# The chunk matrices of the recurrence as 64x64 diagonal blocks, multiplied in quarters of the TensorE array

## What is computed

```python
def step(S, inp):
    r_t, w_t, k_t, v_t, a_t, b_t = inp
    sa = jnp.einsum('bhvk,bhk->bhv', S, a_t)
    S = S * w_t[:, :, None, :] + sa[..., None] * b_t[:, :, None, :] + v_t[..., None] * k_t[:, :, None, :]
    y = jnp.einsum('bhvk,bhk->bhv', S, r_t)
    return S, y
...
_, ys = lax.scan(step, S0, xs)          # 256 steps, 16 heads, S is 64x64 for each head
...
y = ((y - mean) * lax.rsqrt(var + GN_EPS)).reshape(B, T, D_RWKV)
...
return (y + bonus.reshape(B, T, D_RWKV)) * g
```

## Time and profile before

| what | value |
|---|---|
| median of three executions | 2832.23 us (2830.13 to 2838.66) |
| profiled execution: its time | 2842.54 us |
| profiled execution: span of its instructions | 2840.8 us |
| PE busy | 2535.0 us (89% of the span) |
| DVE busy | 1992.4 us (70%) |
| ACT busy | 1122.2 us (40%) |
| granted TensorE clock, mean | 0.938 of 2.4 GHz |

### The profile page before, as it was taken

One profiled execution on the slowest core, in us unless ns is written; L12 is line 12 of the kernel. 1 busy time (PEld: TensorE's weight loads), 2 busy tenths in 40 slices (PEclk: granted clock), 3 DMA queues, 4 the chain that ended last, 5 costly groups with the idle time before them and its releaser, 6 DMA issues.

```text
span 2840.8 us, 49508 instructions
## 1 busy us (share of the span) xinstructions
PE 2535.0 (89%) x20356; PEld 2457.9 (87%) x20356; DVE 1992.4 (70%) x2444; ACT 1122.2 (40%) x1179; POOL 96.5 (3%) x184
## 2 busy tenths in 40 slices
PE   1298996889999999999889998998899999999997
PEld 1298973889999999999788887888899999999997
DVE  6877776578887778777778776866678754465644
ACT  1143332345554324443344343342455543344433
POOL 1000000000000000000000000000000000000000
PEclk7599995999999999999999989999899999999999
DMA  9776860567776877777657231320477545455543
GB/s 385 292 298 252 331 258 15 191 239 271 289 292 261 322 282 285 284 281 286 262 208 268 89 125 36 119 104 20 164 280 269 218 163 187 169 192 180 190 164 117
DMA packets 87613, 613.58 MB, mean 216 GB/s; under 512 B 9545, under 2 KB 13137, under 8 KB 14033
## 3 DMA queue, kind: packets, MB, share of 16 engines
q1 hardware_dynamic: 64320, 443.22, 42.5%
q0 software_dynamic: 23184, 168.83, 15.4%
HBM read 607.80 MB, written 4.21 MB: 215 GB/s over the span
## 4 chain that ended last, share of the span: by engine, by line
PE 81%; DVE 12%; issue 4%; ACT 2%; DMA 0%; DVEq 0%; SPq 0%; ACTq 0%
PE ps L645 23%; PE ps L647 23%; PE ps L646 23%; PE ps L642 1%; PE ps L550 1%; DVE ada_raw L1438 1%; DVE w_lo L1425 1%; DVE inv_t L1339 1%; PE ps L566 1%; DVE tmp L1463 1%; DVE w_lo L1421 1%; DVE h_lo L1467 1%; PE ps L767 1%; DVE rstd L1455 1%; PE ps L447 1%
## 5 line engine op out<-in xcount | busy, mean ns | idle before, releaser
L645 PE MATMUL ps<-h_hi,w_hi 128*128 128x256 f32 x4480 | 1273.1, 284 | 165.7 <-DVE w_lo L1421 111.2
L647 PE MATMUL ps<-h_hi,w_lo 128*128 128x256 f32 x4480 | 1268.3, 283 | 0.0
L646 PE MATMUL ps<-h_lo,w_hi 128*128 128x256 f32 x4480 | 1262.8, 282 | 0.0
L1421 DVE TENSOR_TENSOR w_lo<-w_raw,w_hi 128x2048 fp32r<-128x2048 f32 x323 | 740.2, 2292 | 532.0 <-ACT w_hi L953 531.0
L953 ACT CAST w_hi<-w_raw 128x2048 fp32r<-128x2048 f32 x323 | 617.0, 1910 | 1052.0 <-PE ps L647 1027.6
L645 PEld LDWEIGHTS ps<-h_hi,w_hi 128*128 128x128 f32 x4480 | 857.4, 191 | 173.8 <-issue 143.4
L646 PEld LDWEIGHTS ps<-h_lo,w_hi 128*128 128x128 f32 x4480 | 857.6, 191 | 0.4
L647 PEld LDWEIGHTS ps<-h_hi,w_lo 128*128 128x128 f32 x4480 | 856.3, 191 | 0.0
L645 PE MATMUL ps<-hid_hi,w_hi 128*128 (+1 forms) x1408 | 396.8, 282 | 21.8 <-issue 21.8
L646 PE MATMUL ps<-hid_lo,w_hi 128*128 (+1 forms) x1408 | 397.0, 282 | 0.0
L647 PE MATMUL ps<-hid_hi,w_lo 128*128 (+1 forms) x1408 | 396.2, 281 | 0.0
(11 more groups left out here) (334 smaller groups left out, 1831.2 us busy)
## 6 DMA issues: line engine op xcount, KB each, us to landing
w_raw<-in_w_stream SPq DMA_DIRECT2D x376, 1024.0 KB, 4.8
ada_raw<-in_ada_stream POOLq DMA_DIRECT2D x160, 1024.0 KB, 6.5
w_raw<-in_ada_stream SPq DMA_DIRECT2D x32, 1024.0 KB, 4.8
x<-in_x_t SPq DMA_DIRECT2D x1, 2048.0 KB, 18.2
x_kept<-x SPq DMA_DIRECT2D x1, 2048.0 KB, 8.3
x<-x_kept SPq DMA_DIRECT2D x1, 2048.0 KB, 7.7
out_t<-x SPq DMA_DIRECT2D x4, 512.0 KB, 2.6
ada_c<-in_c SPq DMA_DIRECT2D x1, 1024.0 KB, 4.9
```

Of the source, the lines that this page charges most:

```text
L645: mm(o, hi, r_hi, start=first, stop=False, **kw)
L646: mm(o, hi, r_lo, start=False, stop=False, **kw)
L647: return mm(o, lo, r_hi, start=False, stop=last, **kw)
L1421: tt(w_lo[:, slot], w_raw[:, slot], w_hi[:, slot % 2].bitcast(F32), ALU.subtract).then_inc(lo_ready, 1)
```

## The change

The chunk matrices shrink from 128x128 to two stacked 64x64 blocks (`mats`, `n_low`, `inv`, `inv_t`, and the mask constants). Every matmul on them is cut into matmuls of 64 rows and 64 columns, one for each block (`HALVES`). The products of both heads come in one go, four quarters in turn, so that the PE no longer waits for DVE between the heads. DVE handles all four matrices of a group in one instruction of half the width, and `mats` is masked last, after everything that the first level needs. The transposes move from ahead of level 0 into it, and the `mats` products with the values move from level 4 to level 2. The outputs are 16 quarter matmuls for a group instead of 8 of 128 rows. The sequence over the chunks (5) has the same matmuls as before. Line numbers of the tensor and vector programs move by up to 16.

```diff
-CONSTS = [("ident", 128), ("ones", 128), ("head64", 128), ("low0", 128), ("up0", 128), ("lev", 5 * 128),
-          ("strict_low", 128), ("mask2", 256), ("tri", 256), ("scan", 256), ("recip", 1024)]
+CONSTS = [("ident", 128), ("ones", 128), ("head64", 128), ("low0", 64), ("up0", 64), ("lev", 5 * 64),
+          ("strict_low", 64), ("mask3", 3 * 64), ("ident64", 64), ("tri", 256), ("scan", 256), ("recip", 1024)]
...
-                mats = [sb(t, f"mats{i}", [P, 4, 3, P]) for i in range(2)]
-                n_low = [sb(t, f"n_low{i}", [P, 4, P]) for i in range(2)]
-                inv = [sb(t, f"inv{i}", [P, 4, P]) for i in range(2)]
-                inv_t = [sb(t, f"inv_t{i}", [P, 4, P]) for i in range(2)]
+                mats = [sb(t, f"mats{i}", [P, 4, 3, CHUNK]) for i in range(2)]
+                n_low = [sb(t, f"n_low{i}", [P, 4, CHUNK]) for i in range(2)]
+                inv = [sb(t, f"inv{i}", [P, 4, CHUNK]) for i in range(2)]
+                inv_t = [sb(t, f"inv_t{i}", [P, 4, CHUNK]) for i in range(2)]
...
+        HALVES = [slice(0, 64), slice(64, P)]
+
+        def by_chunk(t):
+            return t.rearrange("p (w t) -> p w t", w=4)
...
-            for e in range(2):
-                rows = slice(64 * e, 64 * e + 64)
-                for s, g, b in both:
-                    BT, KTL = wk[s][:, 5], wk[s][:, 4]
-                    if e:
-                        pe.wait_ge(S("masked"), of(i, 2, 0, s))
-                    else:
-                        pe.wait_ge(S("tilded"), g + 1)
-                    for t in range(2):
-                        tt = slice(P * t, P * t + P)
-                        mm(ps[:, b + t, 0:T], BT[rows, tt], ar[s][rows, :, tt], start=True, stop=True)
-                        mm(ps[:, b + t, T:512], KTL[rows, tt], ar[s][rows, :, tt], start=True, stop=True)
...
+            for s, g, b in both:
+                pe.wait_ge(S("tilded"), g + 1)
+                for t in range(2):
+                    for k, src in ((0, 5), (2, 4)):
+                        for h, p in enumerate(HALVES):
+                            for e, rows in enumerate(HALVES):
+                                tt = slice(P * t + 64 * h, P * t + 64 * h + 64)
+                                o = (4 * t + k) * 64
+                                mm(ps[p, b + e, o:o + P], wk[s][rows, src, tt], ar[s][rows, :, tt], start=True, stop=True)
...
             for m in range(5):
                 for s, g, b in both:
-                    NL = wtmp[s][:, 0:2].rearrange("p a (b t) -> p (a b) t", b=2)
+                    NL = by_chunk(wtmp[s][:, 0])
...
                     for w in range(4):
-                        last = mm(ps[:, b, w * P:w * P + P], NL[:, w], inv_t[s][:, w], start=True, stop=True)
+                        for p in HALVES:
+                            last = mm(ps[p, b + 2, w * 64:w * 64 + 64], NL[p, w], inv_t[s][p, w], start=True, stop=True)
                     last.then_inc(S("half"), 1)
...
+                for k, src, n in ((0, u_tok[s], 0), (1, tok[s][:, 2], 2)):
+                    for t in range(2):
+                        for h, p in enumerate(HALVES):
+                            for e, rows in enumerate(HALVES):
+                                last = mm(ps[rows, b + h, T + t * 64:T + t * 64 + 64], src[p, t, rows],
+                                          mats[s][p, 2 * e + t, n, :], start=k == 0 and t == 0, stop=k == 1 and t == 1,
+                                          skip_group_check=True)
...
-                    nc.scalar.copy(wtmp[s][:, 2:4].rearrange("p a t -> p (a t)"), ps[:, b, :]).then_inc(S("yt"), 1)
...
+                    nc.scalar.copy(wtmp[s][:, 2], ps[:, b + 2, 0:T]).then_inc(S("yt"), 1)
...
-                    last = tt(inv_t[s][:], inv_t[s][:], ps[:, b + 1, :].rearrange("p (w t) -> p w t", w=4), ALU.add)
+                    last = tt(inv_t[s][:], inv_t[s][:], by_chunk(ps[:, b + 1, 0:T]), ALU.add)
```

More of the change, by code:

```diff
@@ L118, in level, with within @@
         return (i // (2 << m) == j // (2 << m)) & (i % (2 << m) >= (1 << m)) & (j % (2 << m) < (1 << m))
[L120 to L125, removed]
+    def within(m):
+        return np.where(i < CHUNK, m[:, :CHUNK], m[:, CHUNK:])
+    put("low0", within(level(0)))
+    put("up0", within(level(0).T))
+    put("lev", np.concatenate([within(level(m)) for m in range(1, 6)], 1))
+    put("strict_low", within(j < i))
+    strict, incl = within(i < j), within(i <= j)
+    put("mask3", np.concatenate([incl, strict, incl], 1))
+    put("ident64", within(i == j))
     put("tri", i <= np.arange(T)[None, :])
@@ L483, in wkv_pe @@
         def wkv_pe(pe, mm, pair, i):
[L484 removed]
+            head64 = wk_const("head64", P)
             both = groups(i)
@@ new lines, in wkv_pe @@
+            for s, g, b in both:
+                pe.wait_ge(S("rk_read"), g + 1)
+            for s, g, b in both:
+                for t in range(2):
+                    for h, p in enumerate(HALVES):
+                        for e, rows in enumerate(HALVES):
+                            tt = slice(P * t + 64 * h, P * t + 64 * h + 64)
+                            o = T + P * s + 64 * t
+                            last = mm(ps[p, 4 + 3 * e, o:o + 64], ar[s][rows, 0, tt], wk[s][rows, 5, tt], start=True,
+                                      stop=True)
@@ L551, in wkv_pe @@
                     last.then_inc(S("half"), 1)
-                if m == 4:
+                if m == 0:
                     for s, g, b in both:
-                        pe.wait_ge(S("inv_ready"), of(i, 5, m, s))
+                        pe.wait_ge(S("masked"), g + 1)
+                        for n, src in enumerate((wk[s][:, 5], wk[s][:, 4])):
+                            for t in range(2):
+                                last = nc.tensor.transpose(ps[:, b, (2 * n + t) * P:(2 * n + t) * P + P],
+                                                           src[:, t * P:t * P + P], ident[:])
+                        last.then_inc(S("tok_turned"), 1)
@@ L556, in wkv_pe @@
+                if m == 2:
+                    for s, g, b in both:
+                        pe.wait_ge(S("tok"), g + 1)
                         for w in range(4):
                             e, t = w // 2, w % 2
-                            last = mm(ps[:, b + 2, (2 * t + e) * 64:(2 * t + e) * 64 + 64], mats[s][:, w, 1, :],
-                                      tok[s][:, 2, t, 64 * e:64 * e + 64], start=True, stop=True)
+                            for p in HALVES:
+                                last = mm(ps[p, b, (2 * t + e) * 64:(2 * t + e) * 64 + 64], mats[s][p, w, 1, :],
+                                          tok[s][p, 2, t, 64 * e:64 * e + 64], start=True, stop=True)
@@ L1326, in wkv_dve, with products @@
-            dve.wait_ge(S("masked"), of(i, 2, 1, 1))
+            def products(b):
+                return ps[:, b:b + 2, :].rearrange("p e (t k j) -> p (e t) k j", t=2, k=4)
+            dve.wait_ge(S("mats_mm"), i + 1)
+            for s, g, b in both:
+                o = T + P * s
+                tt(n_low[s][:].rearrange("p (e t) j -> p e t j", e=2),
+                   ps[:, 4:8:3, o:o + P].rearrange("p e (t j) -> p e t j", t=2),
+                   wk_const("strict_low").unsqueeze(1).unsqueeze(1).to_broadcast([P, 2, 2, CHUNK]),
+                   ALU.mult).then_inc(S("low_read"), 1)
+                steps.add(tt(inv_t[s][:], products(b)[:, :, 0], all4(wk_const("up0")), ALU.mult))
@@ L1333, in wkv_dve @@
             each(lambda s, g, b: tt(inv[s][:], n_low[s][:], all4(wk_const("low0")), ALU.mult))
             for s, g, b in both:
-                tt(inv[s][:], inv[s][:], all4(ident[:]), ALU.add).then_inc(S("inv_ready"), 1)
+                tt(inv[s][:], inv[s][:], all4(wk_const("ident64")), ALU.add).then_inc(S("inv_ready"), 1)
+            for s, g, b in both:
+                tt(mats[s][:].rearrange("p w k j -> p w (k j)"), products(b)[:, :, 1:4].rearrange("p w k j -> p w (k j)"),
+                   wk_const("mask3", 3 * CHUNK).unsqueeze(1).to_broadcast([P, 4, 3 * CHUNK]), ALU.mult).then_inc(S("masked"), 1)
```

87 lines of the change are left out of this document (30 added, 57 removed).

## The result

The median of four executions (one more of the kernel before than in the table above) went from 2834.09 us (2830.13 to 2838.66) to 2765.74 us (2764.61 to 2770.28): 0.9764 of the time before, with a 95% interval of 0.9750 to 0.9778, or 68 us less. The kernel is faster, by twice the 34 us that I forecast, and within the range given (2745 to 2828).

What follows compares the result with a forecast made beforehand. No transfer or single engine bounds the changed stretches; a chain between PE, DVE and ACT does. Head -6.3, levels -3.6, chunks +0.8, outputs -1.7, norm +2.2: -8.6 us a stage, -34 in all, 2798 us; range 2745 to 2828.

Steps and rivals of the forecast that it cites:

- The head: Stage start to first addition to `inv_t`: 6.3 us less a stage; first half at 5.4 us, second product at 9.8.
- the clock in the level loop: Level loop: granted clock taken as half (0.50), making a level 5.5 us, against 3.7 at full clock.
- The two ends: Level loop's clock, all full or all half: four levels sum to 17.2 us or 22.8, instead of 26.4.
- The levels' term: Level loop of each stage: 3.6 us less at half clock, the value taken; 9.2 less at full clock.
- Case (a): Rival for the stages: the clock holds at full, -20.8 us a stage, -83 in all, 2749 us; chance 0.2.
- the main case: All four stages: half clock from head to norm, -8.6 us a stage, 2798 us, spanning 2780 to 2812; chance 0.52.
- Chunks and outputs: Sequence over the chunks +0.8 us a stage, all at half clock; outputs -1.7; together -0.9.
- The norm's term: Norm and the weight unit after it: +2.2 us a stage, from 3 to 5 us at half rate; bounds 0 and +5.
- The weight split: 2.29 us on DVE after levels 1 and 3: at full clock sticks out about 1.0 us, twice; fits beside PE at half.
- Case (b): Rival on PE: passes issued no faster than now, about 0.061 us apart; -0.1 us a stage, 2832 us; chance 0.15.
- Case (c): Rival in the levels: a matrix's two blocks do not run side by side; +11.2 us a stage, +45, 2877; chance 0.1.
- Case (d): Rival: the section gains but under 0.3% reaches the end, half clock lasting through the next weight units; chance 0.03.

Runs made afterwards that it cites:

- e9: Changed kernel with the passes of block 1 left out of levels 1 to 4 (second block's inverse wrong): 2790.82 us, one run.
- e8: Changed kernel with a 128x128x128 f32 matmul of constants, result thrown away, at three places of every chunk step (two in the last): 2765.39 us.
- e12: Changed kernel with masks of `mats` cut by bank, transposes behind the products, second weight split behind the chunks, and quarter-array filler matmuls in chunk steps: 2748.75 us.
- e10: Changed kernel with block 0's passes issued twice and block 1's left out in levels 1 to 4 (second block's inverse wrong): 2794.92 us, one run.
- e5: Changed kernel with the second split of the next stage's weights moved from behind level 3 to behind the chunk loop: 2765.43 us, stretch -4.0 us.
- e3: Changed kernel with every matmul of the level loop issued twice, same operands and output: 2799.07 us, one run.
- e1: Changed kernel with the level loop's four matmuls of block 0 first, then block 1's, instead of in turn: 2778.37 us, one run.
- e4: Changed kernel with the masks of `mats`, the token transposes and their copies put back ahead of the first half-level: 2774.43 us, stretch -0.3 us.

## Why the prediction was right in its direction and half in its size

**The head** was right: +5.4 and +9.9 where I had 5.4 and 9.8, the transposes and the masks as the wait that eats part of the gain, and the half clock there. It gained 5.9 us against the 6.3 forecast.

**The failing step is the clock in the level loop.** I wrote: "The two ends are all full clock and all half clock; I take half, since the nearest row (the chunks) lost it." The level loop ran at 1.00 in all four stages, but for its first 0.3 to 2.1 us. The chunks were no guide to it. By the windows above the levels issue 394 passes in 16.2 us and the chunks 68 in 4.14, while I had only weighed that both work in quarters and that PE is busy all the time. Fewer passes in the same loop did lose the clock (e9), and fillers in the chunks kept it (e8 in all four stages, e12 in three). But e10 kept it with about as many passes per time as the chunks had, so this isn't the whole reason, and the cause stays open. e9's level at half clock took the 5.5 us that I had forecast. So the mechanism and the price of half clock were right, and the choice between the two ends was wrong. My full-clock figures, 3.7 us a level and 17.2 for all four, were measured as 3.72 and 17.0. That the second pair agrees so well is in part chance: one of the two weight splits that I had at 1.0 each cost nothing, while the half clock at the start, which I left out there, added 0.4 in the mean, and the other split cost 1.2. The levels' term alone makes -5.8 a stage, or 23 of the 33 us by which the sum was short.

**Case (a)** was right for the levels alone. Head, chunks and norm had the half clock for a large part of their length, as in the main case, so the time ended between the two, 17 us above (a)'s 2749.

**Chunks and outputs** gained 1.8 and not 0.9, because the first chunk and most of the second still ran at full clock, and I had them at half. **The norm's term** was +0.5 and not +2.2: the half clock ended at 1623.86, 2.3 us after the norm's first matmul, and the weight unit behind the norm took 5.53 us, as before.

**The weight split** was to stick out twice by 1.0 at full clock. It did once. Behind level 1 the level took 4.65 us, 0.93 more than 3.72, which are the two sets of the products with the values; nothing is left for the split, though no run took either of them away. Behind level 3 it cost 1.2 (e5).

**Case (b)**, passes issued no faster than 0.061 us apart, is refuted: the 64 passes of L535 take 1.98 us from first start to last end, 0.031 each, and the 16 of a level's set start within 0.47. The Trainium skill's 62 ns for a MATMUL decoded in microcode and its floor of about 25 ns from start to start (TensorE: Matmul & The Clock Gate, "Wait — 56ns, not 53.3ns?") are both not seen in these bursts. In the trace the passes of L535 start in fours, one in each quarter and 0.007 us apart, with a four every 0.109; so their mean of 0.027 from start to start comes of four quarters at work and is no floor on the issue.

**Case (c)** is refuted by e3 beside e10. Had it held, a level at the granted clock of 1.00 would have taken 5.85 us, +24 us in the stretch against what happened: still faster than before, so my +45 needed the half clock too, which e10 did not have.

**Case (d)** did not occur; what the stages gained reached the end, 66.9 of the 68.4 us of the medians.

## What to carry to other kernels

Cutting masked zero blocks out of matmuls pays most when quarters are issued in turn, so that two of them run side by side: the stretch lost 66.9 us that way, 57.1 with one block ahead of the other (e1), and 43.0 with as many passes for half the blocks, all in one quarter (e10). Price each loop at both clocks, and choose for each loop by itself: the same shape of matmul and a busy engine in another stretch say little of the clock here. After such a cut, look for what used to be hidden: here a 2.29 us vector instruction at the end of a shorter level, and two masks ahead of the transposes, together 13 us of the stretch for two pieces of code in other places.

## What the runs showed of the hardware that I had not expected

- Two quarters of the array on different rows, writing different partitions of one PSUM bank, run fully side by side: 32 passes in 1.10 us, 16 in one of the quarters in 1.09.
- To run fully side by side, the quarters' matmuls must be issued in turn: with eight passes of one quarter ahead of the other's, a set takes 0.96 instead of 0.68 us.
- The clock of a loop did not follow from PE's busy share alone, nor from its passes per time alone: levels in one quarter kept 1.00 with 17.4 passes a microsecond and chunks lost it with 16.4; levels kept it with PE busy for 82% of the time and chunks lost it with 93%.
- A gain in the head can be lost at the other end of a stage through the clock: e4's stages 0 and 1 were 2.0 and 1.6 us ahead at the last level, and stage 0 was 2.4 behind after the next stage's first weight unit.
- A full-array filler between quarter matmuls took 0.42 us, while fillers in quarters (eight passes) left the chunk at 2.45 us (in e12 1610.71 to 1613.16, between the first passes of the second and third chunk), against 2.49 for the changed kernel's first chunk, both at full clock.
